# Recurrent layer on one Trainium2 core: gates by tanh, thirds that run on as their gates come, and two thirds of the out product as split passes

## What is computed

```python
proj = x @ w_in
y_branch, u = jnp.split(proj, 2, axis=-1)
y_branch = jax.nn.gelu(y_branch, approximate=True)
u = causal_conv4(u, conv_w) + conv_b
gates = jnp.einsum('bsnk,gnkj->gbsnj', ub, gate_w) + gate_b[:, None, None]   # 6 blocks of 256
gates = jax.nn.sigmoid(gates)
r, i = gates[0], gates[1]
log_a = -LRU_C * r * jax.nn.softplus(-a_param)        # LRU_C = 8
a = jnp.exp(log_a)
b = jnp.sqrt(-jnp.expm1(2.0 * log_a)) * (i * u)
h_t = a_t * h_(t-1) + b_t                             # along the tokens
m = (h * y_branch) @ w_out                            # 1536 -> 1024
```

## Time and profile before

| | us |
|---|---|
| median of 3 runs | 1549.32 |
| lowest and highest | 1548.64, 1551.37 |
| the profiled execution | 1550.36 |
| its span, first to last instruction | 1548.6 |
| TensorE, VectorE, ScalarE busy | 1450.7, 793.3, 631.3 |

### The profile page before, as it was taken

The page is one execution under the profiler, slowest core; times in us unless marked ns, Lnnn a source line. Parts: engine busy times, 40 slices in busy tenths (PEclk is TensorE's granted clock), DMA queues, the critical chain, the costliest instruction groups (busy, mean ns, idle before and its releaser), DMA issues.

```text
span 1548.6 us, 23407 instructions
## 1 busy us (share of the span) xinstructions
PE 1450.7 (94%) x9844; PEld 1138.0 (73%) x9844; DVE 793.3 (51%) x1104; ACT 631.3 (41%) x889; POOL 105.5 (7%) x77
## 2 busy tenths in 40 slices
PE   7999999999999899999999999899999999899895
PEld 7889789999989688999999988586444334334333
DVE  5557847765469246776457877855122222222223
ACT  5553355344466635544455755553112112112112
POOL 2000001000022003020010001400000000000000
PEclk9999999999999999999999999898999999999997
DMA  9644446545564645455470242045999999999992
GB/s 371 230 180 163 150 168 260 202 174 178 203 258 177 248 187 218 164 182 200 164 280 1 77 171 81 29 164 216 406 427 430 428 427 427 430 428 427 430 429 107
DMA packets 27877, 383.05 MB, mean 247 GB/s; under 512 B 3168, under 2 KB 3296, under 8 KB 4496
## 3 DMA queue, kind: packets, MB, share of 16 engines
q1 hardware_dynamic: 27072, 377.71, 60.9%
q0 software_dynamic: 720, 4.11, 0.7%
HBM read 380.76 MB, written 1.05 MB: 247 GB/s over the span
## 4 chain that ended last, share of the span: by engine, by line
PE 39%; DMA 16%; DVE 7%; ACT 2%; issue 1%; POOL 0%; SPq 0%; ACTq 0%; DVEq 0%; POOLq 0%
PE ps L580 39%; DMA ring<-in_experts 16%; DVE w_lo L1675 2%; DVE work L1687 1%; DVE SQ L1675 1%; ACT work L1199 1%; ACT L1199 0%; ACT w_hi L1199 0%; DVE work L1675 0%; DVE HM L1675 0%; DVE X L1687 0%; DVE cst L1698 0%; DVE act L1675 0%; ACT lr L1199 0%; PE ps L718 0%
## 5 line engine op out<-in xcount | busy, mean ns | idle before, releaser
L1675 DVE TENSOR_TENSOR w_lo<-ring,w_hi 128x1024 fp32r<-128x1024 f32 x264 | 339.8, 1295 | 240.6 <-ACT w_hi L1199 240.5
L580 PE MATMUL ps<-in_hi,w_hi 128*128 128x256 f32 x1376 | 393.7, 286 | 24.2 <-DVE w_lo L1675 18.9
L580 PE MATMUL ps<-in_hi,w_lo 128*128 128x256 f32 x1376 | 389.5, 283 | 0.0
L580 PE MATMUL ps<-in_lo,w_hi 128*128 128x256 f32 x1376 | 389.2, 283 | 0.0
L1199 ACT ACTIVATE w_hi<-ring 128x1024 fp32r<-128x1024 f32 x264 | 277.3, 1055 | 255.3 <-PE ps L580 238.5
L580 PE MATMUL ps<-ring,work 128*64 128x512 f32 (+1 forms) x1568 | 348.2, 591 | 28.0 <-DMA ring<-in_experts 17.0
L580 PEld LDWEIGHTS ps<-ring,work 128*64 128x64 f32 (+1 forms) x1568 | 111.6, 138 | 241.5 <-issue 199.7
L580 PEld LDWEIGHTS ps<-in_hi,w_hi 128*128 128x128 f32 x1376 | 262.1, 190 | 30.5 <-issue 23.3
L580 PEld LDWEIGHTS ps<-in_lo,w_hi 128*128 128x128 f32 x1376 | 262.3, 191 | 0.2
L580 PEld LDWEIGHTS ps<-in_hi,w_lo 128*128 128x128 f32 x1376 | 262.2, 191 | 0.0
L1199 ACT ACTIVATE work<-ps 128x512 f32<-128x512 f32 x64 | 37.7, 594 | 323.8 <-PE ps L1174 190.4
(11 more groups left out here) (265 smaller groups left out, 1988.7 us busy)
## 6 DMA issues: line engine op xcount, KB each, us to landing
ring<-in_experts SPq DMA_DIRECT2D x96, 2048.0 KB, 22.7
ring<-in_dense SPq DMA_DIRECT2D x82, 2048.0 KB, 7.9
ring<-in_dense SPq DMA_DIRECT2D x4, 512.0 KB, 8.6
cst<-in_ret_cst POOLq DMA_DIRECT2D x1, 1280.0 KB, 14.0
X<-in_x SPq DMA_DIRECT2D x4, 256.0 KB, 7.7
cst<-in_ctx POOLq DMA_DIRECT2D x1, 1024.0 KB, 7.6
cst<-in_ssd_cst POOLq DMA_DIRECT2D x1, 1024.0 KB, 5.2
out<-HM SPq DMA_DIRECT2D x1, 1024.0 KB, 3.8
```

The source lines that it names most:

```text
L580: i = pe.matmul(o, l, r, start=start, stop=stop)
L1675: i = dve.tensor_tensor(out=o, in0=x, in1=y, op=op)
```

## The change

Gates: a sigmoid is written as (1 + tanh(x/2)) / 2. ScalarE takes tanh with the scale 0.5 and a halved bias (half_bias); the constants of the decays become 4 times softplus with a bias of the same size (sp4, nsp4), the product with i becomes (li + 1) * u, and the root gets the factor 0.25. Tanh stands in the same table as gelu and as exp.

Order: with the first two groups of gates read, ScalarE makes the first third's decays, and so on in turn (gate_tiles, decays, root); VectorE follows with arguments and scans. Modulation 5 moves between the gates, unit and tile too; the column sums of modulation 7 move behind the first third of the out product.

Out product: the first third stays plain and reads uc. The second and third are split: ScalarE and VectorE split the product of each (third_hi, third_lo) and eight chunks of weights; the last third is laid out by _third_blocks so that its chunks go bank by bank.

```diff
           ("mod", 1, 2), ("ffn_in0", 0, 11), ("ffn_out0", 0, 6), ("mod", 3, 2), ("lru_u", 0, 3), ("lru_y", 0, 3),
-          ("lru_gate", 0, 2), ("mod", 5, 3), ("lru_out", 0, 3), ("mod", 8, 2), ("ffn_in1", 0, 11),
+          ("lru_gate", 0, 1), ("mod", 5, 1), ("lru_gate", 1, 1), ("mod", 6, 2), ("lru_out", 0, 3), ("mod", 8, 2), ("ffn_in1", 0, 11),
           ("ffn_out1", 0, 6), ("mod", 10, 2), ("ssd_b", 0, 1), ("ssd_xs", 0, 2), ("ssd_c", 0, 1), ("ssd_f", 0, 1),
...
 _tiles("lru_u", KL // 2)
 _tiles("lru_y", KL // 2)
-_tiles("lru_gate", KL)
-_mod(5, 6, 7)
+for _i in range(KL):
+    if _i == KL // 2:
+        _mod(5)
+    _seq.append(("lru_gate", _i))
+_mod(6, 7)
 _tiles("lru_out", 4)
...
 
         sq2, scaled_up = at(6180, KD, T), at(13312, 2, T)
-        upad, uc, gy, li = at(0, KL, LPAD + T), at(3108, KL, T), at(6180, KL, T), at(9252, KL, T)
...
-        sp8, nsp8 = small[:, 96:96 + KL], small[:, 108:108 + KL]
+        lr_tail = at(12328, KL - KD, T)
+        sp4, nsp4 = small[:, 96:96 + KL], small[:, 108:108 + KL]
         lsp = at(120, 3, KL, of=small)
+        half_bias = small[:, 504:504 + 2 * KL]
+        go_hi, go_lo = over("work", 0, "go_hi", KL, T), over("work", 9256, "go_lo", KL, T)
 
...
                             mm(bank(t)[:, m * T:(m + 1) * T], w[:, b * P:(b + 1) * P], uc[:, 2 * n + c, :], c == 0,
                                c == 1, bank_full[t % ROT] if m == 1 and c == 1 else None)
-            mod_rows(5)
+                if n == 2:
+                    mod_rows(5)
+                if n == 4:
+                    mod_cols(5)
             mod_rows(6)
-            mod_cols(5)
             mod_rows(7)
             mod_cols(6)
-            mod_cols(7)
...
                 w = weights("lru_out", n)
-                pe.wait_ge(s["go_ready"], n + 1)
+                if n == 0:
+                    pe.wait_ge(s["g_done"], 1)
+                else:
+                    pe.wait_ge(s["go_ready"], n)
                 for b in range(4 * KD):
                     c, m = (b // KD, b % KD) if n < 2 else (b % 4, b // 4)
                     t = TILE["lru_out", m // 2]
+                    o = bank(t)[:, m % 2 * T:(m % 2 + 1) * T]
+                    if n == 0:
+                        mm(o, w[:, b * P:(b + 1) * P], uc[:, c, :], c == 0 and m % 2 == 0, False)
+                        continue
+                    ch = CHUNK_AT["lru_out"][0] + 4 * (n - 1) + b // BPC
+                    if b % BPC == 0:
+                        chunk_begin(ch)
+                    wh, wl = (x[:, b % BPC * P:(b % BPC + 1) * P] for x in (part_hi(ch), part_lo(ch)))
                     last = n == 2 and c == 3 and m % 2 == 1
-                    mm(bank(t)[:, m % 2 * T:(m % 2 + 1) * T], w[:, (c * KD + m) * P:(c * KD + m + 1) * P], li[:, 4 * n + c, :],
-                       n == 0 and c == 0 and m % 2 == 0, last, bank_full[t % ROT] if last else None)
+                    mm(o, wh, go_hi[:, 4 * n + c, :], False, False)
+                    mm(o, wh, go_lo[:, 4 * n + c, :], False, False)
+                    mm(o, wl, go_hi[:, 4 * n + c, :], False, last, bank_full[t % ROT] if last else None)
+                if n == 0:
+                    mod_cols(7)
             next_input(3, "ffn_in1", (8, 9))
             ffn(1)
             chunk_end()
...
             gelu(KL // 2 - 1)
-            for n in range(KL // 2):
+            act.wait_ge(s["lsp_dve"], 3)
+
+            def gate_tiles(n):
+
                 for gate in range(2):
                     t = TILE["lru_gate", 2 * n + gate]
                     await_full(act, t)
                     for m in range(2):
                         i = 2 * n + m
                         o = (r_tiles(i) if gate == 0 else li[:, i:i + 1, :]).rearrange("p a b -> p (a b)")
-                        fn(o, bank(t)[:, m * T:(m + 1) * T], ACT.Sigmoid, bank_read[t % ROT] if m == 1 else None,
-                           bias=col("lgate_b", gate * KL + i))
-            act.wait_ge(s["lsp_dve"], 3)
-            await_read(act, TILE["lru_gate", KL - 1])
-            await_read(act, TILE["lru_gate", KL - 2])
-            for n in range(3):
-                for i in range(4 * n, 4 * n + 4):
+                        fn(o, bank(t)[:, m * T:(m + 1) * T], ACT.Tanh, bank_read[t % ROT] if m == 1 else None,
+                           scale=0.5, bias=half_bias[:, gate * KL + i:gate * KL + i + 1])
+
+            def decays(k):
+
+                await_read(act, TILE["lru_gate", 4 * k])
+                await_read(act, TILE["lru_gate", 4 * k + 2])
+                for i in range(4 * k, 4 * k + 4):
                     fn(la[:, i, :], r_tiles(i)[:, 0, :], ACT.Exp, s["a_ready"] if i % 4 == 3 else None,
-                       scale=nsp8[:, i:i + 1])
-                if n == 0:
-                    mod_read(5)
-                    mod_read(6)
-                act.wait_ge(s["a_ready"], n + 1)
-                for i in range(4 * n, 4 * n + 4):
+                       scale=nsp4[:, i:i + 1], bias=nsp4[:, i:i + 1])
+                act.wait_ge(s["a_ready"], k + 1)
+                for i in range(4 * k, 4 * k + 4):
                     fn(r_tiles(i)[:, 0, :], r_tiles(i)[:, 0, :], ACT.Tanh, s["th_ready"] if i % 4 == 3 else None,
-                       scale=sp8[:, i:i + 1])
-                if n == 0:
-                    mod_read(7)
-                act.wait_ge(s["lsq_arg"], n + 1)
-                u4 = uc[:, 4 * n:4 * n + 4, :].rearrange("p a b -> p (a b)")
-                fn(u4, u4, ACT.Sqrt, s["lsq_ready"])
-            weights_hi(CHUNK_AT["ffn_in1"][0] + 2)
-            mixer_out("lru_out")
+                       scale=sp4[:, i:i + 1], bias=sp4[:, i:i + 1])
+
+            def root(k):
+                act.wait_ge(s["lsq_arg"], k + 1)
+                u4 = uc[:, 4 * k:4 * k + 4, :].rearrange("p a b -> p (a b)")
+                fn(u4, u4, ACT.Sqrt, s["lsq_ready"], scale=0.25)
+
+            def third_hi(k):
+                act.wait_ge(s["g_done"], k + 1)
+                fn(go_hi[:, 4 * k:4 * k + 4, :], uc[:, 4 * k:4 * k + 4, :], ACT.Copy, s["go_hi_ready"])
+
+            lo0 = CHUNK_AT["lru_out"][0]
+            act.wait_ge(s["uc_ready"], KL)
+            gate_tiles(0)
+            gate_tiles(1)
+            decays(0)
+            gate_tiles(2)
+            root(0)
+            mod_read(5)
+            gate_tiles(3)
+            decays(1)
+            gate_tiles(4)
+            gate_tiles(5)
+            mod_read(6)
+            decays(2)
+            mod_read(7)
+            weights_hi(lo0 + 2)
+            root(1)
+            root(2)
+            third_hi(1)
+            weights_hi(lo0 + 3)
+            third_hi(2)
+            weights_hi(lo0 + 6)
+            mixer_out("lru_out", lambda j: weights_hi(lo0 + 7 + j))
             next_input(3, "ffn_in1", (8, 9))
             ffn(1)
             inv_rms(7)
...
+            settle(ts(nsp4, ap, -1.0, MUL))
+            log1p_begin(lsp[:, 1, :], sp4)
+            log1p_end(lsp[:, 0, :], lsp[:, 1, :], lsp[:, 2, :], nsp4, sp4)
+            settle(ts(sp4, sp4, 4.0, MUL))
+            ts(half_bias, col("lgate_b", 0, 2 * KL), 0.5, MUL)
+            ts(nsp4, sp4, -1.0, MUL, inc=s["lsp_dve"])
             weights_lo(chunks_by("ret_v", 2))
             dve.wait_ge(s["ld_ret"], 16)
             tt(cut(rcos, 2, T), cut(rcos, 2, T), rstd2, MUL)
...
                 return v[:, 4 * n:4 * n + 4, :]
 
-            await_read(dve, TILE["lru_gate", KL - 1])
-            dve.wait_ge(s["uc_ready"], KL)
-            for n in range(3):
-                x = tt(four(li, n), four(li, n), four(uc, n), MUL)
-            settle(x)
-            for n in range(3):
-                dve.wait_ge(s["a_ready"], n + 1)
-                settle(tt(four(uc, n), four(la, n), four(la, n), MUL))
-                dve.wait_ge(s["th_ready"], n + 1)
-                stt(four(uc, n), four(uc, n), 1.0, r_tiles(4 * n, 4), ADD, MUL, s["lsq_arg"])
-                dve.wait_ge(s["lsq_ready"], n + 1)
-                settle(tt(four(li, n), four(li, n), four(uc, n), MUL))
-                for i in range(4 * n, 4 * n + 4):
+            def arguments(k):
+
+                await_read(dve, TILE["lru_gate", 4 * k + 1])
+                await_read(dve, TILE["lru_gate", 4 * k + 3])
+                settle(stt(four(li, k), four(li, k), 1.0, four(uc, k), ADD, MUL))
+                dve.wait_ge(s["a_ready"], k + 1)
+                settle(tt(four(uc, k), four(la, k), four(la, k), MUL))
+                dve.wait_ge(s["th_ready"], k + 1)
+                stt(four(uc, k), four(uc, k), 1.0, r_tiles(4 * k, 4), ADD, MUL, s["lsq_arg"])
+
+            def scans(k):
+
+                dve.wait_ge(s["lsq_ready"], k + 1)
+                settle(tt(four(li, k), four(li, k), four(uc, k), MUL))
+                for i in range(4 * k, 4 * k + 4):
                     x = dve.tensor_tensor_scan(uc[:, i, :], la[:, i, :], li[:, i, :], 0.0, MUL, ADD)
                 settle(x)
-                if n == 0:
+                if k == 0:
```

(33 more changed lines are left out.)

9 lines of the change are left out of this document (2 added, 7 removed).

## The result

The changed kernel takes 1534.97 us (median of 4 runs, 1533.49 to 1535.11); the kernel before took 1548.98 beside it. The ratio is 0.9906, with a 95% interval of 0.9895 to 0.9918, so 14.0 us or 0.94% less. The forecast was 1535.0. That it fits so closely is partly luck, as the layer itself gained less than forecast.

The account below looks back on a forecast made before the run. TensorE, busy 94% of the span, was taken as the bound, with idle time and low clock around the out product. Terms 6.9 + 2.9 + 4.7 - 0.8 gave 13.7, 14.8 with overlap; 14.3 taken: 1535.0 us, range 1533.5 to 1538 (80%).

Parts of the forecast that it names:

- Bound and idle time: Ahead of the out product, TensorE's 6.35 us idle mostly goes and one column sum moves: 6.9 us net gain.
- Clock: In the out product, the half-speed clock behind the idle time goes: 2.9 us gain.
- Passes: In the out product, 64 of 96 blocks go from 0.431 to 0.357 us as split passes: 4.7 us gain.
- Waits: In the out product's later thirds, TensorE waits 0.8 us at full durations, for the fourth chunk of weights.
- timetable: Recurrent layer's new order laid out by engine, each instruction at full duration: out product starts at 534.5, ends at 573.0.
- The sum: Whole layer: 6.9 + 2.9 + 4.7 - 0.8 = 13.7 us gain, 14.8 with overlap; 14.3 taken.
- part 2: Idle time and clock ahead of the out product: ScalarE's new order timed, out product starting at 534.5 at full clock.
- timetable with overlap: Recurrent layer with ScalarE's neighbouring instructions overlapping: the 0.3 and most of the 0.8 us waits go, gain 14.8 us.
- Late ScalarE: Rival ahead of the out product: table switches cost twice 1.28 us, modulation 6 is 3.8 us late; 1540.5 or 1543.4, 11%.
- Given back: Rival behind the layer: a transfer in the experts or next-layer work, formerly covered, takes back the gain; 1549.3, 3%.
- conversion's pace: Rival in the out product: conversion and split passes do not overlap, 17.4 us more; 1552.4, 3%.

Follow-up runs that it names:

- the experiment that changed nothing else: Kernel before, with 14 products into a bank nobody reads added in the idle time ahead of the out product: 1546.2 us, ratio 0.9981.
- the rearranged kernel: Changed kernel with column sums 6 behind the out product's first third, roots before weight conversion, fourth chunk converted earlier: 1534.6 us, 1535.11 when repeated.

## Why the prediction was right, and where it was off

**Bound and idle time.** The reading that TensorE's idle time in front of the out product and the low clock behind it were the cost of waiting held. Idle time in the stretch was 7.26 us and is 0.71: 6.55 gained. The forecast had 6.9 net, its start of the out product at 534.5 with the gates at 505.91, so 28.6 us behind them; measured were 534.21 - 505.18 = 29.0.

**Clock.** Forecast 2.9 us, measured 2.8 in the experiment that changed nothing else. The wait of 0.71 us left the clock at 1.00, as the forecast had it from the row with 0.91. But the margin was small: in the kernel with the split passes alone a wait of 1.22 us at that place lost it.

**Passes.** Forecast 64 x 0.074 = 4.7 us. The later thirds take 27.7 us plain and 573.27 - 549.47 = 23.8 us split, of which 0.66 is the wait: 27.7 - 23.14 = 4.6. The Trainium skill, page "FP8 and Floating Point Precision", section "TensorE Precision Notes", says that true FP32 makes four passes; an estimate by it, three quarters of the time for three passes, would have been 6.9 us. This case's traces do not agree: 23.14 / 27.7 is 0.84.

**Waits.** Forecast 0.8 us at full durations or nearly none; measured 0.42 + 0.66. The fourth chunk waits where the forecast had it, 0.66 us instead of 0.8. The second third's lower half, which the timetable had ready 0.2 us ahead of need, came 0.42 late.

**The sum.** 6.55 + 2.8 + 4.6 - 1.08 = 12.9 against a measured 12.7. The forecast took 14.3, between 13.7 and 14.8. Without the bias the layer gains 14.9, so the timetable with overlap was the right end, and one of its terms was too small: "four exp 1.71, four tanh 1.71" in part 2, and with it the eight decays of each later third. The diff shows a bias beside each scale, and I costed the new instruction with the row of the old. It took 2.1 us; the choice of the middle gave 0.5 back. The Trainium skill, page "ScalarE: Activation LUTs", section "What ACT_TABLE_LOAD costs", says that each per-partition pointer operand adds about 93 ns to an activation. The trace agrees: (2.07 - 1.71) / 4 = 0.09. The prediction drew on this section for its table loads alone.

**The missing 1.3 us.** The median gained 14.0, the layer 12.7. In the profiled executions the rest comes from outside: the gates began 0.7 us earlier, 0.6 of which is there within the first 46 us (a row of TensorE at 45.14 us before is at 44.54 now), and 1.8 us lie behind the layer. Of these 1.6 fall into one stretch, where the clock was low in one execution and not in the other (below). The span of the one profile is so 15.3 us shorter, more than the median. No run shows that the change causes this, so the last 1.3 us are luck as far as is known, and they made the forecast look better than its working was.

**Late ScalarE.** Its mechanism showed in small: the chain of the thirds had no slack left, and 2.2 us of length came out as 2.1 us of time. Its cause as I put it, switches that cost twice their row, is not there: the gates in front of the load of 513.14 end 0.01 us ahead of it, and the decays start 0.02 us behind its 1.28 us. The Trainium skill, page "ScalarE: Activation LUTs", section "What ACT_TABLE_LOAD costs", adds some 1380 ns of drain to a switch; this case's traces do not agree, for none of the four switches shows it. ScalarE makes these four between the gelu and the last root, where it made seven before.

**Given back, and conversion's pace.** Neither came. The chain's first piece that waits for an expert moved with everything else, from 1211.22 to 1195.73 us, and in the layer no engine waited for a transfer. No chunk waited behind the fourth, and with double work on VectorE TensorE did not wait from the fifth on either.

## What to carry to other kernels

When an edit changes the form of an instruction and not only its place, cost the new form: an operand more on each of 24 small instructions used up the whole slack of a chain that three engines share. A TensorE that is nearly always busy need not set the pace: ask the chain which engine does. Idle time on TensorE costs more than its length where the clock falls behind it, so look for work that can be moved into or behind the gap, even work of 1 us; moved the wrong way it cost 5. And measure an edit by the length of its own stage in several traces, for a saving of 1.6 us in the stage was plain there and invisible in the medians.

## What the runs showed of the hardware

The clock doesn't follow from the idle time in front alone. Two rows from the state-space mixer of the last block, a timeline row and the stretch behind it, in the kernel before:

```profile
967.24 2.21 PE L580 MATMUL ps<-HM,work 128*64 128x256 f32 x16 [1.25 <-DVE HM L1675]
968.00:970.00 2.00, 2.00 (x15) 1.53 (x12) 1.97 (x5) 1.33 (x2) 1.26 (x2) 0.50 1.07 455
```

and in the changed kernel, at the same place of the program, whose code the change doesn't touch:

```profile
953.68 1.52 PE L585 MATMUL ps<-HM,work 128*64 128x256 f32 x16 [1.25 <-DVE HM L1722]
954.40:956.40 2.00, 2.00 (x22) 1.41 (x18) 1.97 (x5) 1.33 (x2) 1.26 (x2) 1.00 1.03 442
```

TensorE had stood idle for 1.25 us in both, with the same products in front. In one the clock fell to 0.50 and in the other it stayed at 1.00, and the difference is worth 1.6 us there. Over the twelve traces several stretches of this sort, always at the same places, are slow in some executions and not in others, in the two profiles of the rearranged kernel too. A little further on, a wait of 3.25 us kept the clock at 1.00 in three of the twelve traces and lost it in the others. In the recurrent layer idle times of up to 0.91 us kept the clock in every trace, 1.22 us lost it in the one in which it occurred, and 1.89, 3.48 and 6.35 lost it. But 1.65 us between split passes, in the kernel with VectorE's work doubled, kept it, and so did 1.69 us in front of the next feed-forward layer in all twelve. So the length of the gap alone does not decide. What does is left open by these runs.
